# One unrolled program in place of ten barriered bodies; V rows gathered by token and summed on TensorE with 128x32 operands, U and V gathers in groups of four

## The reference, cut to what matters

```python
q = (xb @ w_q).reshape(PEER_TB, PEER_HEADS, 2, PEER_DQ // 2)
s = jnp.einsum('thcd,cnd->thcn', q, keys32)
sv, si = lax.top_k(s, PEER_TOPK)
...
a = jnp.einsum('thkd,td->thk', jnp.take(u_tab, e, axis=0), xb)
wgt = gate * jax.nn.gelu(a, approximate=False)
return jnp.einsum('thk,thkd->td', wgt, jnp.take(v_tab, e, axis=0))
```

## Time and profile before

| | us |
|---|---|
| median of 3 runs (lowest to highest) | 4379.45 (4377.17 to 4383.8) |
| the profiled execution's own time | 4385.39 |
| span of its trace, first to last instruction | 4383.6 |
| busy: DVE / PE / POOL / ACT | 3325.8 / 2950.1 / 2723.0 / 854.8 |
| DMA: bytes moved, mean rate over the span | 1454.21 MB, 332 GB/s |
| mean granted clock of TensorE | 0.828 of full speed |

### The profile page before, as it was taken

The page is one execution under the profiler, slowest core; times in us unless marked ns, Lnnn a source line. Parts: engine busy times, 40 slices in busy tenths (PEclk is TensorE's granted clock), DMA queues, the critical chain, the costliest instruction groups (busy, mean ns, idle before and its releaser), DMA issues. The chain is left out here.

```text
span 4383.6 us, 39840 instructions
## 1 busy us (share of the span) xinstructions
PE 2950.1 (67%) x12882; PEld 2000.8 (46%) x12882; DVE 3325.8 (76%) x6429; ACT 854.8 (19%) x1663; POOL 2723.0 (62%) x2350
## 2 busy tenths in 40 slices
PE   6736566765777666776588577867578575756456
PEld 5634353543455444554365345545355344534222
DVE  3487878777977888687878887687868795787764
ACT  2112111311122112221122112221122112211111
POOL 1046766587657756676657766676657664686574
PEclk9878787977888788988898798888788787878778
DMA  5269998989899998999898989999898989999896
GB/s 181 92 247 358 338 381 312 406 305 361 335 372 350 342 392 322 379 320 378 303 393 327 357 344 359 360 325 376 316 403 306 366 339 267 375 318 362 276 387 241
DMA packets 388059, 1454.21 MB, mean 332 GB/s; under 512 B 64528, under 2 KB 67536, under 8 KB 353296
## 3 DMA queue, kind: packets, MB, share of 16 engines
q0 software_dynamic: 313344, 1140.99, 70.4%
q1 hardware_dynamic: 73200, 305.92, 18.1%
q10 hardware_dynamic: 1312, 4.72, 0.3%
HBM read 1441.69 MB, written 9.51 MB: 331 GB/s over the span
## 5 line engine op out<-in xcount | busy, mean ns | idle before, releaser
L491 POOL DMA_INDIRECT ring<-peer_u,idx_c x1061 | 1292.9, 1219 | 791.9 <-DVE dots L1432 415.6
L1432 DVE CUSTOM_DVE_ANT_0 ring<-ring,xn_c 128x1024 f32<-128x1024 f32 x1088 | 1333.0, 1241 | 497.3 <-DMA ring<-peer_u,idx_c 447.0
L1039 PE MATMUL bank<-ring,diag 128*128 128x512 f32 x1920 | 1172.6, 748 | 795.5 <-DMA ring<-peer_v,idx_c 709.8
L491 POOL DMA_INDIRECT ring<-peer_v,idx_c x1088 | 1223.2, 1124 | 580.5 <-issue 275.1
L1039 PEld LDWEIGHTS bank<-ring,diag 128*128 128x128 f32 x1920 | 413.0, 233 | 1335.2 <-DMA ring<-peer_v,idx_c 894.0
L1440 DVE SCALAR_TENSOR_TENSOR h_c<-ring,wgt,h_c 128x1024 f32<-128x1024 f32 x608 | 807.2, 1328 | 215.6 <-DMA ring<-peer_v,idx_c 206.5
L803 PEld LDWEIGHTS bank<-aT,wring 128*128 128x128 f32 x4608 | 566.7, 203 | 118.6 <-issue 41.4
L803 PE MATMUL bank<-aT,wring 128*128 128x128 f32 x4608 | 572.8, 287 | 64.8 <-DVE aT L1077 27.0
L807 PE MATMUL bank<-wring,aT 128*128 128x256 f32 (+1 forms) x1440 | 348.6, 400 | 32.5 <-DVEq L1314 15.2
L807 PEld LDWEIGHTS bank<-wring,aT 128*128 128x128 f32 x1440 | 288.6, 203 | 107.8 <-issue 61.8
L759 ACT ACTIVATE diag<-ident,wgt 128x128 f32<-128x128 f32 x480 | 179.1, 393 | 373.0 <-PE bank L1039 287.2
(11 more groups left out here) (264 smaller groups left out, 3097.1 us busy)
## 6 DMA issues: line engine op xcount, KB each, us to landing
wring<-w_pieces SPq DMA_DIRECT2D x252, 1024.0 KB, 8.3
wring<-w_pieces SPq DMA_DIRECT2D x18, 1056.0 KB, 8.5
ring<-peer_v,idx_c POOLq DMA_INDIRECT x1088, 6.4
ring<-peer_u,idx_c POOLq DMA_INDIRECT x1061, 6.8
wring<-w_pieces SPq DMA_DIRECT2D x18, 512.0 KB, 6.9
x<-x_prompt SPq DMA_DIRECT2D x8, 512.0 KB, 4.4
out_y_prompt<-arena ACTq DMA_DIRECT2D x8, 512.0 KB, 8.9
out_k_prompt<-kst SPq DMA_DIRECT2D x8, 256.0 KB, 8.7
```

The costliest lines, as they stand in the source:

```text
L491: pool.indirect_dma_start(out=ring[0:rows, n % RING, :], out_offset=None, in_=t["peer_" + kind], in_offset=bass.IndirectOffsetOnAxis(ap=id ...
L1039: last = pe.matmul(YB[g][0:peer, :], diag[0:peer, m % DIAGS, 0:peer], ring[0:peer, r, 512 * g:512 * g + 512], start=(m == 0), stop=(m == l ...
L1432: v.tensor_tensor_reduce(out=row, in0=row, in1=xn_c[0:peer, :], scale=1.0, scalar=0.0, op0=ALU.mult, op1=ALU.add, accum_out=dots[0:peer, k ...
```

## The change

The program becomes one block without loops and without barriers or semaphore clears between tiles: a function `at` works out the value that a semaphore will have, and every wait names it. There are 12 steps of 68 slots. In step s stand the front of tile s, the U picks of tile s-1, the V rows of tile s-2 and the tail of tile s-3; so the U and the V of one tile are a whole step apart. Each gather's place in the program is written out by `GATHERS`:

```diff
-RING = 8
-AHEAD = 3
+RING = 10
+QUAD = 32
+VST = 4
+SLOTS = 68
+HEAD = 4
+OVER = 2 * HEAD
...
+def v_tokens(t, s):
+
+    n = rows_of(t)
+    if t == LAST:
+        return (HEAD, 0, n) if s == t + 2 else (0, n, n)
+    return (HEAD, 0, n - OVER) if s == t + 2 else (0, n - OVER, n)
...
+        for _j in range(u_picks(_s - 1) if _s - 1 <= LAST else 0):
+            _step[HEAD + _j // 2].append(("u", _s - 1, _j))
...
+    for _k in range(1, len(_step), 2):
+        _both = _step[_k - 1] + _step[_k]
+        _step[_k - 1] = [e for e in _both if e[0] == "u"]
+        _step[_k] = [e for e in _both if e[0] == "v"]
```

```diff
-                                    for g in range(2):
-                                        last = pe.matmul(YB[g][0:peer, :], diag[0:peer, m % DIAGS, 0:peer],
-                                                         ring[0:peer, r, 512 * g:512 * g + 512],
-                                                         start=(m == 0), stop=(m == len(sched.tensor) - 1))
-                                    last.then_inc(consumed[r], 1)
+                def weighted(i, tokens):
+
+                    q, n_tok = quads_of(i), rows_of(i)
+                    for n in tokens:
+                        wait_landed(pe, NUMBER["v", i, n])
+                        if n == 0 and i >= 1:
+                            pe.wait_ge(*till("h2_ready", i - 1))
+                        if n % q == 0 or n == tokens[0]:
+                            pe.wait_ge(*till("vst_ready", i, n // q + 1))
+                    for g in range(2):
+                        for n in tokens:
...
+                            last = pe.matmul(YB[g][QUAD * j:QUAD * j + QUAD, :], vst[:, slot, j, :],
+                                             ring[:, r, 512 * g:512 * g + 512],
+                                             start=(n // q == 0), stop=(n // q == n_tok // q - 1))
+                            if g == 1:
+                                last.then_inc(consumed[r], 1)
...
-                                v.scalar_tensor_tensor(out=h_c[0:peer, :], in0=row, scalar=wgt[0:peer, k:k + 1],
-                                                       in1=h_c[0:peer, :], op0=ALU.mult, op1=ALU.add)\
-                                    .then_inc(consumed[r], 1)
+                def stationary(i, m):
...
+                    v.tensor_tensor(vst[:, n % VST, 0:q, :], bcast(columns, QUAD),
+                                    over(unit[:, QUAD - 1 - m:2 * QUAD - 1 - m], q), ALU.mult)\
+                        .then_inc(S["vst_ready"], 1)
```

The normed row that the dots need stands in two PSUM banks (`XN`, copied there by ACT) instead of SBUF:

```diff
-                                v.tensor_tensor_reduce(out=row, in0=row, in1=xn_c[0:peer, :], scale=1.0, scalar=0.0,
+                    v.tensor_tensor_reduce(out=ring[:, r, :], in0=ring[:, r, :], in1=XN[:], scale=1.0, scalar=0.0,
```

2362 lines of the change are left out of this document (1215 added, 1147 removed).

## The result

| | before | after |
|---|---|---|
| median, us (lowest to highest, runs) | 4381.62 (4377.17 to 4388.66, 4) | 4219.52 (4209.29 to 4226.44, 4) |
| profiled execution's own time / span, us | 4385.39 / 4383.6 | 4214.92 / 4211.9 |
| ratio, 95% interval | | 0.9627 (0.9601 to 0.9653) |

A forecast was written before the change was run, and what follows sets the result against it. No engine fills a step; the bound changes inside it: DMA near its ceiling, POOL in slots 22 to 53, DVE in the choice. Steps of 460 us plus fronts, sample and tail sum to 4227, stated 4225 us, range 4030 to 4550.

The forecast's parts named there:

- 143, 195, 101, 21: Forecast us of a full step: slots 4 to 21, slots 22 to 53, choice of experts, gates to first dots.
- this case: The main forecast for the whole kernel, 4225 us, with measured times from 4110 to 4340 counted to it; chance 0.50.
- 4.4 us a group: TensorE's sixteen V instructions for four tokens: the middle between 1.9 us with strips abreast and 7.0 in sequence.
- a drain: Cost on TensorE of changing tiling mode: 0.15 us, two in a group, 10 us in a step.
- its two bounds: POOL's time for 128 gathers in slots 22 to 53: 159 to 186 us.
- the third rival: POOL freed and DMA at its ceiling, 178 us in slots 22 to 53; kernel 4010 us; chance 0.13.
- the second rival: Groups of four in lock-step: blocked buffers stop POOL, slots 22 to 53 stay at 216 us; kernel 4480; chance 0.20.
- the half-way value: Slots 22 to 53 taken at 195 us, half way from DMA's 178 to the earlier 216.
- ten buffers: Argument against the lock-step of groups of four: the ring has ten buffers; that case had chance 0.20.
- The first rival: TensorE takes the strips one after another, 7.0 us a group, 212 us in slots 22 to 53; kernel 4780; chance 0.17.
- The choice and the start: Slots 54 to 67, set by DVE, 101 us; from the gates to the next first dots, 21 us.
- the swap's 44 us: Extra time of the sample's step for swapped state and caches; half removed by an earlier start, leaving 480 us.

The follow-up runs named there:

- e10: Changed kernel with token and bank loops exchanged, so TensorE waits for and frees one token's rows at a time: 4106.6 us, ratio 0.9381.
- e6: Changed kernel with gathers not joined over slot pairs, so TensorE sums two tokens at a time instead of four: 4064.7 us, ratio 0.9287.
- e7: Changed kernel with a ring of 8 gathered-row buffers instead of 10: 4677.1 us, ratio 1.0689.
- e1: Changed kernel with all four tokens of most groups written to one strip instead of four: 4554 us, one run.
- e2: Changed kernel with the normed row that the dots read in SBUF instead of PSUM: 4299.9 us, ratio 0.9837.
- e12: Changed kernel with the inverse's seven mask products on POOL again instead of DVE: 4198.2 us, ratio 0.9567.
- e3: Changed kernel with U picks moved out of the choice, V groups redistributed and 12 stationary blocks instead of 4: 4199.7 us, ratio 0.9611.
- e5: Changed kernel with no V rows held back for the next step's start: 4195.1 us, ratio 0.9566.
- e4: Changed kernel with the state and convolution-row transfers moved earlier in SP's queue: 4186.3 us, ratio 0.9576.

## Why the prediction was right, and where it wasn't

**The mechanism and the sum.** The order of the stretches, their owners and their sizes came out: 143, 195, 101, 21 against 139, 195, 99, 16. The chances put 0.50 on this case, and the time is in the middle of it. The sum was off by 15 us because its misses cancel: steps 1 to 6 took 77 us less than forecast and the sample's step took 8 us less, but the first front, step 7 and the last part 70 us more. That the total is so near is luck.

**Slots 22 to 53: the right number, with two of its causes mis-sized.** TensorE was taken at 171 us with 4.4 us a group, and measured 135 with 2.95 on average over the kernel and 1.92 at the full clock: the lower bound of the term, not its middle. Its other part was too high as well: the V groups took 44 us there and the stages 88 on average over steps 3 to 6, where the sum had 70 and 100. At the full clock the four strips are 16 x 0.437 / 1.92 = 3.6 times as fast as one after another. The Trainium skill, "TensorE: Matmul & The Clock Gate", section Part 3, has 2.38 for three tiles, from which the prediction's estimate of 2.9 us a group came; that the average is so near to it is chance, since it mixes groups at both levels of the clock. What the prediction calls a drain (0.15 us) is only what a single instruction takes more than one in a row; a change of mode doesn't show in the time of a group: the one at 3133.95 us of the changed kernel, with stage work right before and behind it, takes 1.92 us like those that stand alone.

POOL came out at the lower of its two bounds (124 us busy and, by its waits in that stretch, 34.8 of issue: 159). By both, the stretch should have gone to 178, the third rival. What stood between was the second rival's wait, 39 us of POOL's time in the stretch shown, which the text had set on top of 195, at 216. So the rival named the right wait and gave it the wrong place in the sum: it was inside the half-way value, not above it. The forecast had named this wait too, but nothing in it gave the half; that 195 was hit to the us is luck. Nor is the wait all of it: e10 and e6, which loosen it, take 113 and 155 us off the kernel but only 4 and 7 off this stretch (191 and 187 us on average), and what keeps it above 178 even then is open. The rival's "ten buffers" against itself was right as well: with eight the kernel takes 4677 us (e7).

**The first rival** fell by the trace, and e1 shows that its price was real: 7.2 us a group and a kernel that is slower than before.

**POOL and the dots' operand.** The gathers fell to 0.96 us, and e2 gives back the V gathers' part of that wholly, the U gathers' by half, and 80 us of the kernel's time. The cost falls on POOL alone, 0.14 to 0.17 us a gather. The Trainium skill, "SBUF — State Buffer", section Who interferes with whom, says that a DVE instruction with two SBUF inputs contends with a GpSimd instruction that reads SBUF; e2 agrees as far as POOL's gathers go. What the prediction listed as taken off POOL, its products, was worth nothing: e12 shows nothing lost with the masks on POOL.

**The choice and the start.** DVE is the owner of the choice (93 of 98 us; e3 takes it to 64 to 68). In the start, 21 was taken, 16 measured, and 9 without the held rows (e5): the wait was for the rows put there as a cover.

**The fixed parts.** Step 7 (+27) is the term that was mis-sized most in a step: the forecast moved half of the swap's 44 us of the earlier trace rows into the sample's step, and the trace shows most of it in step 7, in SP's queue; e4 takes 33 us off. The V rows of the sample by themselves took 124 us instead of 96; the tail of tile 7 with its five pieces, 13 us of DMA, stands in the same 124 us, and the sum had charged pieces one step earlier only. What the other 15 are is not settled. The first front ended at 267 instead of 256; 6 of the 11 us are the masks on DVE (e12).

**What no run undoes.** The barriers, the V sums on DVE, the attention over each tile's own blocks and the trip of `h1` to HBM were not put back one by one, so what each of them is worth in the 162 us isn't shown.

## What to carry to other kernels

If a group of instructions waits for several transfers and frees their buffers together, count the buffers that it holds while it waits; waiting and releasing one by one can be worth more than the time that the grouping saves on the engine. Relieving an engine that is not full can be worth nothing (the masks, e12) or 80 us (the dots' operand, e2), so undo each part of a change by itself. Moving work out of a bound stretch pays only as far as the stretches that take it have buffers and room: here such moves gave from almost nothing to some 70 us, by where the gathers went and by the size of the groups beside them. A few transfers of single elements belong where their queue waits anyway.

## What was not expected of the hardware

- Two strips cost as much as four: 8 instructions in 1.91 us (e6) and 16 in 1.92, at a granted clock of 1.00; on one strip a group of 16 costs 7.2 us on average.
- The granted clock followed TensorE's own work: 0.787 with four abreast, 0.853 with added instructions that compute nothing, 0.881 in twos, 0.905 on one strip. Work that was added to TensorE cost less than its time (e1), and with the filler cost nothing; how much of that is the clock and how much TensorE's idle time is not parted.
- A dot with both inputs in SBUF is not slower itself (1.224 us against 1.219), but the gathers beside it are (1.10 to 1.13 us against 0.96, e2).
- Three transfers of single elements hold SP's queue for 30 us (e4), and the loads behind them wait.
- A share of DMA of 0.99 is not its ceiling: 380 GB/s in the changed kernel and 409 in twos stand beside 0.99 and 1.02.
